# A decoder layer on eight cores: new order of the last seven-product multiplication, norm passes moved between the engines

## The reference, cut to what matters

```
hcat = x @ w_in                                   # conv B, C, h | retention q, k, v, g
y_conv = b_gate * causal_short_conv(c_gate * hc, conv_w)
q, k = rotary(q), rotary(k) * D**-0.5
y_ret = silu(g) * head_group_norm(chunkwise_retention(q, k, v))
mix = concat(y_conv, y_ret) @ w_out
x = layer_norm(ALPHA * x + mix, ln1_w, ln1_b)     # the first norm
ff = square(relu(x @ w_ff1)) @ w_ff2              # 1024 -> 4096 -> 1024
ple = sigmoid(x @ w_ple_gate) * (p @ w_ple_proj)
x = layer_norm(ALPHA * x + ff + ple, ln2_w, ln2_b)
```

## Time and profile before

| what | value |
|---|---|
| median of 6 runs | 839.18 us (838.46 to 839.75) |
| profiled execution | 839.32 us |
| its span on the slowest core (core 4) | 837.8 us, first to last instruction |
| spans of the eight cores | 833.4 to 837.8 us |
| PE busy | 774.1 us, 92% of the span, 3960 matmuls |
| DVE busy | 543.5 us, 65% |
| ACT busy | 267.1 us, 32% |
| POOL busy | 210.9 us, 25% |
| chain that ended last | PE 79%, DVE 7%, issue 6% |

### The profile page before, as it was taken

The page is one execution under the profiler, slowest core; times in us unless marked ns, Lnnn a source line. Parts: engine busy times, 40 slices in busy tenths (PEclk is TensorE's granted clock), DMA queues, the critical chain, the costliest instruction groups (busy, mean ns, idle before and its releaser), DMA issues.

```text
span 837.8 us, 12281 instructions; the slowest of 8 cores (833.4 to 837.8 us)
## 1 busy us (share of the span) xinstructions
PE 774.1 (92%) x3960; PEld 363.5 (43%) x3960; DVE 543.5 (65%) x767; ACT 267.1 (32%) x495; POOL 210.9 (25%) x220
## 2 busy tenths in 40 slices
PE   3999999999999978989999999999999999999950
PEld 1444445554554433434444444454444444444420
DVE  4556855556854854663358886816764367887997
ACT  2222236555565246453332000124453332000021
POOL 9000036544264433430100000103350100000075
PEclk9999999999999999999999999999999999999995
DMA  9995042300114694685650604677887830522022
GB/s 129 167 189 128 26 126 43 60 26 26 51 51 152 107 167 113 140 178 101 104 98 1 126 10 92 114 163 161 201 210 182 144 58 1 101 51 51 1 101 100
DMA packets 21662, 84.88 MB, mean 101 GB/s; under 512 B 2656, under 2 KB 4832, under 8 KB 16224
## 3 DMA queue, kind: packets, MB, share of 16 engines
q0 software_dynamic: 11088, 52.43, 37.4%
q1 hardware_dynamic: 10368, 31.40, 11.2%
q10 hardware_dynamic: 144, 0.26, 0.1%
HBM read 122.89 MB, written 13.63 MB: 163 GB/s over the span
## 4 chain that ended last, share of the span: by engine, by line
PE 79%; DVE 7%; issue 6%; POOL 2%; DMA 2%; ACT 2%; DVEq 0%; ACTq 0%; POOLq 0%
PE ps L178 77%; DMA xT_56<-xT 2%; PE ps L182 2%; DVE xacc L185 1%; DVE ycat L185 1%; DVE lnst L1047 1%; ACT sqj L207 1%; POOL st_51 L185 1%; DVE ring_111 L185 1%; POOL xtmp L185 0%; DVE ra_77 L185 0%; DVE ring_110 L185 0%; POOL wc_59 L220 0%; DVE ra_78 L185 0%; POOL wc_60 L220 0%
## 5 line engine op out<-in xcount | busy, mean ns | idle before, releaser
L185 DVE TENSOR_TENSOR xacc<-xacc,ps 128x512 f32<-128x512 f32 x80 | 53.4, 683 | 39.7 <-PE ps L178 38.0
L178 PE MATMUL ps<-ring_105,ycat 128*128 128x512 bf16 x288 | 67.1, 379 | 1.0 <-DVE xacc L185 1.0
L207 ACT ACTIVATE xacc<-xacc,lnst 128x1024 f32<-128x1024 f32 x19 | 21.8, 1150 | 124.8 <-POOL lnst L185 107.9
L178 PE MATMUL ps<-ycat,ring_106 128*128 128x512 bf16 x256 | 58.0, 386 | 1.4 <-ACT ycat L207 1.4
L185 DVE TENSOR_TENSOR hT<-ps,tR_136 128x512 bf16<-128x512 f32 x42 | 28.9, 688 | 41.5 <-ACT tR_136 L207 41.5
L185 DVE TENSOR_TENSOR hT<-ps,tR_135 128x512 bf16<-128x512 f32 x43 | 29.6, 688 | 37.2 <-ACT tR_135 L207 37.2
L185 POOL TENSOR_TENSOR lnst<-lnst,neghalf 128x1 f32<-128x1 f32 x32 | 24.6, 775 | 105.7 <-DVE lnst L688 53.7
L185 DVE TENSOR_TENSOR hT<-ps,tR_137 128x512 bf16<-128x512 f32 x43 | 29.6, 689 | 33.0 <-ACT tR_137 L207 33.0
L185 DVE TENSOR_TENSOR ycat<-hT 128x2048 bf16<-128x2048 bf16 x40 | 48.9, 1222 | 2.5
L207 ACT ACTIVATE ycat<-ps 128x1024 bf16<-128x1024 bf16 x16 | 16.4, 1022 | 94.1 <-PE ps L182 94.1
L178 PE MATMUL ps<-ring_104,ycat 128*128 128x512 bf16 x192 | 44.4, 379 | 0.0
(11 more groups left out here) (304 smaller groups left out, 1500.5 us busy)
## 6 DMA issues: line engine op xcount, KB each, us to landing
out<-xacc SPq DMA_DIRECT2D x15, 512.0 KB, 2.8
ring_106<-w_ff POOLq DMA_DIRECT2D x6, 1024.0 KB, 10.4
ring_107<-w_ff POOLq DMA_DIRECT2D x5, 1024.0 KB, 12.0
ring_104<-w_ff POOLq DMA_DIRECT2D x5, 1024.0 KB, 8.4
xtmp<-x SPq DMA_DIRECT2D x8, 512.0 KB, 6.1
ring_108<-w_ff POOLq DMA_DIRECT2D x4, 1024.0 KB, 10.1
ring_109<-w_ff POOLq DMA_DIRECT2D x4, 1024.0 KB, 11.9
ring_105<-w_ff POOLq DMA_DIRECT2D x4, 1024.0 KB, 14.1
```

Of the source, the lines that this page charges most:

```text
L178: self.P.op("pe", lambda e: e.matmul(out, lhsT=lhsT, rhs=rhs, start=start, stop=stop, skip_group_check=skip), reads, writes)
L185: self.P.op(eng, lambda e: e.tensor_tensor(out=out, in0=in0, in1=in1, op=op), reads, writes)
L207: self.P.op("act", lambda e: e.activation(out=out, in_=in_, func=func, **kw), reads, writes)
```

## The change

**The order in the last pass** (s = 1) becomes M1, M2, M3, M6, M4, M5, M7 with its own table of signs, scratch places and PSUM banks; the first pass keeps its table. The code of `phase_ff2` becomes `phase_ff2_first` and `phase_ff2_last`. In the last pass blocks 4 to 7 are complete after the fifth product, and blocks 0 to 3 after the seventh. The weight block "21" is loaded into the free half of `ycat` when M3 begins; before, its two parts went into the places of the weight sum "S", in M3 and M6.

**The second norm of the last pass**: statistics are two ACT passes over each 128x512 half with an accumulated sum (of x/1024 and of x squared/1024), put together by three small DVE instructions; both full passes are DVE's (in halves for blocks 2 and 3). ACT's scaling and POOL's additions are gone.

**The first norm and `gen_out`**: always two DVE passes; `lanes` are gone, so norms run one after another. For blocks 0 to 3 (`fine`) the power is a piece of its own. The flush at column group 16 is replaced by a wait (in the order of the lists) for one block's norm at each pair of column groups. The bf16 copies of blocks 4 and 5 are made during `mix_part` of blocks 8 to 15, and those of 6 and 7 after the first two groups of `phase_ff1`. `mix_part` of blocks 8 to 15 uses all eight PSUM banks instead of four.

**The retention loop**: `do_y` stands behind the projection of k, and its POOL product (`do_ymul`) behind `do_o`.

```diff
-PRODS = dict(
+PRODS = (dict(
...
+), dict(
+    M1=(((0, 0), (1, 1), 1), (((0, 0), 1), ((1, 1), 1)), False),
+    M2=(((0, 1), (1, 1), 1), (((1, 0), 1), ((1, 1), -1)), False),
+    M3=(((0, 0),), (((0, 1), 1),), False),
+    M6=(((0, 1), (0, 0), -1), (((1, 1), 1),), True),
+    M4=(((1, 1),), (((0, 0), 1), ((1, 0), 1)), False),
+    M5=(((0, 0), (1, 0), 1), (((0, 1), 1),), False),
+    M7=(((1, 1), (1, 0), -1), (((0, 0), -1),), True),
+))
...
-        def gen_ln(buf, rbuf, w_t, b_t, rw, rb, slot, spread=True):
+        def gen_ln(buf, rbuf, w_t, b_t, rw, rb, slot, fine=False):
...
-                yield
+                if fine:
+                    yield
...
-            h.act(buf, buf, AF.Copy, [rbuf, rr], [rbuf], scale=rstd)
-            yield
-            h.tt("pool", buf, buf, b_t[:], ALU.add, [rbuf, rb], [rbuf])
+            h.stt(buf, buf, rstd, b_t[:], ALU.mult, ALU.add, [rbuf, rr, rb], [rbuf])
             yield
...
-            if 0 <= t - 2 < NB:
-                do_y(t - 2)
             bg.step()
             if t < NB:
                 do_rot(t, 1)
             elif t == NB:
                 filler()
+            if 0 <= t - 2 < NB:
+                do_y(t - 2)
...
                 do_o(t - 1)
+            if 0 <= t - 2 < NB:
+                do_ymul(t - 2)
...
-                mix_part(b, hf, wo[hf][0], wo[hf][1], next_bank())
-                bg.step(2)
+                mix_part(b, hf, wo[hf][0], wo[hf][1], bank8())
+                bg.step()
+                if chains[4] not in bg.gens and not cast4:
+                    x1_cast(4)
+                    cast4.append(4)
...
-                if s_ == 0 and g == 4:
-                    bg.flush()
...
+                        if s_ == 0 and fc >= 16:
+                            bg.until(chains[8 + (fc - 16) // 2])
...
                         if s_ == 0 and g == 0 and a == 0:
-                            bg.until(chains[4 + f])
-                            x1_cast(4 + f)
                             x1_transpose(4 + f, 4 + f, bank8())
-                        bg.step(3 if s_ == 0 else 2)
+                            if f < 2:
+                                bg.until(chains[6 + f])
+                                x1_cast(6 + f)
+                        bg.step()
...
+                if at_ == ("M3", 0):
+                    for j in range(2):
+                        load_w(s_, 2 + j, j, "21")
...
+            for k, (fn, sc) in enumerate(((AF.Copy, 1.0 / D), (AF.Square, D ** -0.5))):
+                h.act(sg[k][:], v, fn, [("xa", b)], [("sg", k, 1), ("lnst", b)], scale=float(sc),
+                      accum=lnst[:, b, 2 * hf + k:2 * hf + k + 1])
...
+            for v, cols, r in parts:
+                h.stt(v, v, ms[:, 0:1], lnt[2][:, cols], ALU.subtract, ALU.mult,
+                      [rb, ("ms", b), "ln2w"], [r])
```

More of the change, by code:

```diff
@@ L729, in gen_ln1 @@
         def gen_ln1(b):
-            yield from gen_ln(x1v(b), x1r(b), lnt[0], lnt[1], "ln1w", "ln1b", b % 8, b >= 4)
+            yield from gen_ln(x1v(b), x1r(b), lnt[0], lnt[1], "ln1w", "ln1b", b % 8, b < 4)
         def x1_cast(b):
@@ L845, in build_nc @@
         prefetch(6)
+        cast4 = []
         for b in range(8, 16):
             for hf in range(2):
[L848 to L849 removed]
+                mix_part(b, hf, wo[hf][0], wo[hf][1], bank8())
[3 more added lines that the diff above has]
+                    cast4.append(4)
+                elif chains[5] not in bg.gens and len(cast4) == 1:
+                    x1_cast(5)
+                    cast4.append(5)
         for b in range(8, 16):
[L851 removed]
+            chains.append(gen_norm1(b))
+            bg.add(chains[b])
         def phase_ff1(s_):
@@ L954, in ff2_add, with load_w, ff2_product, ff2_adds @@
                  [RP[bank], ("xa", b)], [("xa", b)])
-        def phase_ff2(s_):
-            last = s_ == 1
-            slab_n["use"] += 4
-            WB = dict(M1="S", M5="22", M3="S", M6="12", M2="11", M4="12", M7="S")
-            bg.lanes = 1
+        def load_w(s_, g, j, blk_):
+            t, r = wslot(s_, j, blk_)
+            h.dma("pool", t, w_ff2[g], ("wx", blk_, j), [], r)
+        def ff2_product(s_, m, j, p):
+            si, rs = wslot(s_, j, PLACE[s_][m])
+            bank = BANK[s_][m] + p
+            onto = PRODS[s_][m][2]
+            for k in range(8):
+                c = j * 8 + k
+                lt, rl = left(s_, m, c, p)
+                h.mm(ps[bank][:], lt, si[:, k, :], c == 0 and not onto, c == 15, rl + rs,
+                     [RP[bank]], skip=onto)
+        def ff2_adds(s_, m, p):
+            for (a, hf), sign in PRODS[s_][m][1]:
+                ff2_add(4 * a + p, hf, BANK[s_][m] + p, sign)
+        JP = [(j, p) for j in range(2) for p in range(4)]
+        PJ = [(j, p) for p in range(4) for j in range(2)]
+        def phase_ff2_first():
+            s_ = 0
             def before(m, i):
@@ L988, in before @@
                     bg.step(2)
-                if last:
-                    return
                 if at_ == ("M4", 1):
@@ L1040, in phase_ff2, with phase_ff2_last, before @@
-            bx[0] = 3
+            for m in PRODS[s_]:
+                for i, (j, p) in enumerate(PJ if m in ("M4", "M7") else JP):
+                    before(m, i)
+                    ff2_product(s_, m, j, p)
+                    bg.step(2)
+                    if j == 1:
+                        ff2_adds(s_, m, p)
+                if m != "M4":
+                    bg.flush()
+            bx[0] = 3
+        def phase_ff2_last():
+            s_ = 1
+            sums = {}
+            def before(m, i):
+                at_ = (m, i)
+                if at_ == ("M1", 0):
+                    for j in range(2):
+                        load_w(s_, 4 + j, j, "12")
+                    bg.add(wsum(s_, 1, "S", "11", "22", ALU.add))
+                    bg.add(hsum(s_, "M2"))
+                if at_ == ("M2", 2):
+                    bg.add(wsum(s_, 0, "S", "12", "22", ALU.subtract))
+                    bg.add(wsum(s_, 1, "S", "12", "22", ALU.subtract))
+                if at_ == ("M3", 0):
+                    for j in range(2):
+                        load_w(s_, 2 + j, j, "21")
+                    bg.add(wsum(s_, 0, "12", "12", "11", ALU.add))
+                    bg.add(wsum(s_, 1, "12", "12", "11", ALU.add))
+                    bg.add(hsum(s_, "M6"))
+                if at_ == ("M6", 0):
+                    bg.add(wsum(s_, 0, "11", "21", "11", ALU.subtract))
+                    bg.add(wsum(s_, 1, "11", "21", "11", ALU.subtract))
+                    bg.add(wsum(s_, 0, "S", "21", "22", ALU.add))
+                    bg.add(wsum(s_, 1, "S", "21", "22", ALU.add))
+                if at_ == ("M4", 0):
+                    for q_ in ("M5", "M7"):
+                        sums[q_] = hsum(s_, q_)
+                        bg.add(sums[q_])
+            for m in ("M1", "M2", "M3", "M6", "M4"):
+                for i, (j, p) in enumerate(JP if m in ("M1", "M2", "M3") else PJ):
+                    before(m, i)
+                    ff2_product(s_, m, j, p)
+                    bg.step(2)
+                    if j == 1:
+                        ff2_adds(s_, m, p)
+                        if m == "M6":
+                            last_stats(4 + p, 1)
+                        if m == "M4":
+                            last_stats(4 + p, 0)
+                            bg.add(gen_last(4 + p))
+                if m != "M4":
+                    bg.flush()
+            bg.until(sums["M5"])
+            for m in ("M5", "M7"):
+                bg.until(sums[m])
+                for p in range(4):
+                    for j in range(2):
+                        ff2_product(s_, m, j, p)
+                        if j == 1:
+                            ff2_adds(s_, m, p)
+                            last_stats(p, 1 if m == "M5" else 0)
+                            if m == "M7":
+                                bg.add(gen_last(p))
+                        bg.step(2)
```

153 lines of the change are left out of this document (56 added, 97 removed).

## The result

| what | before | after |
|---|---|---|
| median | 839.16 us (20 runs) | 803.88 us (10 runs, 803.36 to 804.79) |
| ratio after / before | | 0.958, 95% interval 0.9572 to 0.9588 |
| span of the profiled execution | 837.8 us (core 4) | 802.7 us (core 7) |
| PE busy | 774.1 us, 92% | 768.2 us, 96% |
| DVE, POOL busy | 543.5, 210.9 us | 555.8, 144.6 us |

The account below looks back on a forecast made before the run. PE was taken as busy throughout in undisturbed MLP stretches, losing time at four places, the last after its final matmul. Gains of 8.9 + 6.9 + 3 + 14.7 = 33.5 us off 839.32 gave a forecast of 805.7 us, range 798 to 817.

Parts of the forecast that it names:

- (a): Start of the first MLP product: making the bf16 copies earlier removes most PE waits there, gaining 8.9 us.
- (c): Retention loop: waits for masked scores and `ob` go, new waits for psT come, a gain of 3 us.
- (b): Norms of blocks 8 to 15: with ACT and POOL out and blocks spread, PE's waits for hT go, gaining 6.9 us.
- (d): Last pass, fifth product to the end: new order and DVE passes at 1.28 us gain 14.7 us.
- its lower end: Low case of (d): dependent instructions, small ones and waits cost 6 us more, leaving a gain of 8.5 us.
- DVE as the bound of the first norms: Rival: DVE, needing 8.1 of 8.6 us, stays the bound in the first norms; 814.6 us, chance 0.14.
- Latency-bound last norms: Rival: in the last norms the chain ACT, DVE, POOL, DVE is paid at several blocks; 811.9 us, chance 0.12.
- "21" late: Rival: in the last pass weight block "21" lands 5 us late or M4 starves; 810.7 us, chance 0.03.
- Slow passes without POOL: Rival: norm passes stay slow for a cause other than POOL's addition; 862.6 us, chance 0.05.

Follow-up runs that it names:

- first_spread: Changed kernel with the second pass of the norms of blocks 8 to 15 back on ACT and POOL, still one step a group: 805.55 us.
- first_three: Changed kernel with three norms at a time, three steps a group and the mid-phase flush in the first pass, passes staying on DVE: 814.79 us.
- first_fast: Changed kernel with three steps a group in the first pass, one norm at a time, no flush, passes on DVE: 825.84 us.
- first_both: Changed kernel with the edits of first_spread and first_three together: 820.03 us.
- old_paced: old_last with the new pace (one norm at a time, two steps for each half product), old order and old norms: 818.95 us.
- norms_only: old_last with the new norms (statistics on ACT, both passes on DVE), old order and old pace: 823.72 us.
- norms_paced: norms_only with the new pace (one norm at a time, two steps for each half product), old order: 809.34 us.
- old_last: Changed kernel with the whole last pass as before (product order, norms and pace): 819.76 us.

## Why the prediction was right, and where its reasons were not

**Right in size and cause.** (a): 8.9 forecast, 8.7 between the traces, 9.8 when undone alone; the last wait stayed, 1.75 us for the 1.85 forecast. (c): 3 forecast, 3.7 and 4.1 found. The waits for PT went (3.2 us) and those for psT came (2.6 us) as the text had them; of 1.9 us of waits for `ob` 1.0 went, as forecast, and one of 0.9 stayed at the drain. Two errors of the sum cancel. The four starts behind psT are 0.80 to 0.85 us late, 3.3 us in all and not 2.6, because the 0.17 us that the prediction adds to other waits belongs to these too; and some 1.5 us came from waits too short to be listed, which the text named without a size.

**(b): right in size, wrong in cause.** The step that failed is "takes both slow engines out of this chain and spreads the blocks one by one": it gives one sum to two things and sees the cause in the first, the slow engines. That one is worth 1.7 us (first_spread); with the engines as changed, three steps a group, three norms at a time and the flush lose 10.9 (first_three), and three steps a group alone 22 (first_fast). The chain in the earlier trace rows is real, but at one step a group it costs PE nothing: first_spread has it, and no wait for hT. That the size came out is no proof of the cause: 6.9 us was all that PE lost in that stretch, and any cure would have returned it. DVE's filling of 94% (8.1 of some 8.6 us), which the prediction took as the risk, did no harm at the new pace; the trace has DVE busy some 80% there. The rule of the Trainium skill that was weighed there ("Perfetto Trace Analysis", "Optimizing Scalar/DVE Operations") says that moving work between GpSimd and DVE may not help; for the engines alone the runs nearly agree at the new pace, 1.7 us, and less so at the old one, 5.2 (first_both less first_three), while the term as a whole came to 6.9. What three norms at a time, or the flush alone, would do at one step a group wasn't tried.

The undone terms add up to 9.8 + 16.1 + 4.1 + 15.9 = 45.9 us for a saving of 35.3. Most of the surplus is in first_both, where a fast pace loses the early copies of (a) again, 7.7 us of waiting in place of 1.7.

**(d): right in size, the pacing wrong.** Forecast were 56.5 us from the fifth product to the end, measured 55.3, and errors cancel in it. Additions cost 0.60 and passes 1.19 us from start to start (753.39 to 754.59 for two, 761.92 to 763.11) rather than the 0.68 and 1.28 of the rows, whose ends overlap the next start, 2.7 us less over sixteen of each; dependent instructions cost more than counted, 0.17 us of waiting ahead of several second passes and 1.02 us instead of 0.74 for the first small chain (760.90 to 761.92). Two of the text's own sums are slightly off: eight hT pieces of 1.30 us are 10.4 and not 10.2, and the items of its lower end (40 times 0.1, 2 and 2) add up to 8 us and not 6. The waits for ACT were forecast at 2.5 and 0.5 us and came at 2.56 and 0.47. Wrong is the sentence "there the pace is that of the second norm's passes". The slow passes of the earlier trace rows are real, but old_paced has most of them at 1.28 us and is only 0.8 us faster: by the traces the pace was POOL's loop of addition, power and ACT's scaling, 5.3 us a block. The new norms end that loop, but by themselves they put another in its place, DVE, ACT, DVE, POOL, 6.1 us a block (norms_only). So the norms need the pace (norms_paced, 14.4 us better), and the order adds 5.5 us on top. The gain of 15.9 can't be shared out further: alone on old_last the order brings 9.2, the pace 0.8, and the norms lose 4.

**The rivals.** DVE as the bound of the first norms: not at this pace, at three steps a group 11 to 22 us. Latency-bound last norms: true for two blocks, and for all eight in the old order at the old pace. "21" late: its pair landed in time, and no wait for it shows. Slow passes without POOL: none. The 28 full passes with ln2w and ln2b take 1.28 us in the mean, twelve of them in the last pass with ACT's statistics beside them. The only slow full passes of that trace are four with ln1b in the retention loop, 1.97 to 2.03 us: where the change moved them, they start 0.3 to 0.4 us behind POOL's rotary sum of q (1.26 us). No wait of PE names them; whether its 0.3 us for POOL's k hang on one is not shown.

## What to carry to other kernels

Before moving work to another engine, look at where its steps stand in the in-order lists: how many steps are issued for each unit of the main work can decide more than which engine has them. In the first norms the pace was worth 11 to 22 us and the engines 2 to 5 at an equal pace. In the last norms neither helped alone (the pace 0.8 us, the engines a loss of 4), and together they brought 10.4. A dependent step wants other work between itself and what it waits for; where none is left, each wait is paid by all that stands behind. And a loop through two engines, such as a small power behind a long addition, shows in the period from block to block (5.3 us here), not in the busy time of any one engine.

## What the runs showed of the hardware

POOL and DVE hold each other up by whole instructions, either way round. The power of 128x1 takes 0.54 us by itself and 1.46 when it starts under a pass of DVE, which stays at 1.28:

```profile
762.15 1.46 POOL L185 TENSOR_TENSOR lnst<-lnst,neghalf 128x1 f32<-128x1 f32 x1 [40.63 <-DVE lnst L192]
766.38 0.54 POOL L185 TENSOR_TENSOR lnst<-lnst,neghalf 128x1 f32<-128x1 f32 x1 [2.77 <-DVE lnst L192]
```

These are two powers of the changed kernel, the first begun 0.23 us after the pass at 761.92, the second with an addition from PSUM on DVE. POOL's addition is 2.34 us first in line and 3.23 behind a pass (old_paced at 777.10), DVE's pass 1.28 first in line and 3.38 behind an addition. The Trainium skill ("SBUF — State Buffer", "Who interferes with whom") has this as a lock that goes to whoever issues first; these rows agree.

At the first product of the MLP all eight cores kept a granted clock of 1.00 behind a wait of 1.75 us (changed kernel); behind one of 2.0 us (on each of the eight PE starts 2.18 or 2.19 us late) five of eight show 0.88 to 0.90 between 306 and 320 us (first_spread). They had the lower of the two levels for a part of it: on core 3 seven matmuls of 512 columns start 0.43 us apart, twice the 0.213 of the earlier trace rows. It cost each of the five some 1.7 us. Three cores kept 1.00 behind the same wait, so its length alone does not decide.
